# Attention scores and decay tiles contracted over all 128 rows, with one mask product for each tile

## The reference

```python
# mLSTM, 4 heads of 128 channels, chunks; here as one causal 256 x 256 weight
w = jnp.exp(d - m_t[..., None])              # d: sums of gate logs, -inf above the diagonal
qk = jnp.einsum('bhtd,bhsd->bhts', qj, kj) * w
# differential attention, 16 heads of 64 channels, in pairs
s = jnp.einsum('bhqd,bhkd->bhqk', qi, k_sh)
s = jnp.where(key_pos[None, :] <= qpos[:, None], s, -jnp.inf)
a = jax.nn.softmax(s, axis=-1)
diff = a[:, :, 0] - lam * a[:, :, 1]
```

## Time and profile before

| | |
|---|---|
| median of 3 runs | 2908.33 us (2906.72 to 2909.06) |
| span of the profiled execution, first to last instruction | 2907.0 us |
| the profiled execution's own time | not given apart from the span |
| TensorE busy | 2854.6 us (98%), 17894 products |
| VectorE, ScalarE, GpSimd busy | 67%, 56%, 12% |
| chain that ended last | TensorE 90%, VectorE 6%, ScalarE 2%, DMA 1% |
| granted TensorE clock, mean | 0.994 |

### The profile page before, as it was taken

How to read it: one execution, slowest core, us unless ns; L and a number is a source line. 1 busy time by engine, 2 the same in 40 slices (tenths; PEclk the granted TensorE clock), 3 DMA queues, 4 the chain that set the end, 5 groups by cost and what they waited for, 6 DMA issues and landing times.

```text
span 2907.0 us, 44463 instructions
## 1 busy us (share of the span) xinstructions
PE 2854.6 (98%) x17894; PEld 2553.7 (88%) x17894; DVE 1950.4 (67%) x3362; ACT 1633.4 (56%) x2794; POOL 342.4 (12%) x310
## 2 busy tenths in 40 slices
PE   8999999999989999999999999999999999999999
PEld 7888888788868877799999999999888889989997
DVE  6656765765566656759864898777555566756775
ACT  6544654754546555456655445776445555655663
POOL 0000000000000002000001444896000000000000
PEclk9999999999989999999999999999999999999999
DMA  6554556466334555445355554334555574526454
GB/s 211 195 175 152 177 196 210 135 206 217 126 116 151 202 187 163 130 141 176 102 164 183 178 185 162 131 131 159 189 193 198 188 238 133 163 85 209 147 188 153
DMA packets 304540, 490.33 MB, mean 169 GB/s; under 512 B 10880, under 2 KB 236544, under 8 KB 295632
## 3 DMA queue, kind: packets, MB, share of 16 engines
q1 hardware_dynamic: 303200, 480.09, 50.2%
q0 software_dynamic: 1136, 7.41, 0.7%
HBM read 485.36 MB, written 2.10 MB: 168 GB/s over the span
## 4 chain that ended last, share of the span: by engine, by line
PE 90%; DVE 6%; ACT 2%; DMA 1%; issue 1%; POOL 0%; SPq 0%; DVEq 0%; POOLq 0%; ACTq 0%
PE ps L608 30%; PE ps L538 11%; PE ps L542 11%; PE ps L539 11%; PE ps L687 10%; PE ps L686 5%; PE ps L559 2%; PE ps L1123 2%; DVE halves L1369 2%; PE ps L1158 1%; PE ps L1178 1%; PE ps L491 1%; DVE AR L2223 1%; PE ps L842 0%; DVE R L1369 0%
## 5 line engine op out<-in xcount | busy, mean ns | idle before, releaser
L2579 ACT ACTIVATE halves<-raw 128x1024 fp32r<-128x1024 f32 (+1 forms) x842 | 878.6, 1052 | 692.0 <-PE ps L608 335.8
L1369 DVE TENSOR_TENSOR halves<-raw,halves 128x1024 fp32r<-128x1024 f32 (+1 forms) x806 | 964.6, 1218 | 221.6 <-ACT halves L2579 218.8
L538 PE MATMUL ps<-XX,halves 128*128 128x256 f32 (+1 forms) x2360 | 586.5, 286 | 0.0
L539 PE MATMUL ps<-XX,halves 128*128 128x256 f32 (+1 forms) x2360 | 578.2, 283 | 0.0
L608 PE MATMUL ps<-halves,XX 128*128 128x512 f32 x2256 | 524.1, 392 | 5.5 <-DVE XX L1407 2.9
L608 PEld LDWEIGHTS ps<-halves,XX 128*128 128x128 f32 x2256 | 423.4, 189 | 100.3 <-issue 7.9
L538 PEld LDWEIGHTS ps<-XX,halves 128*128 128x128 f32 (+1 forms) x2360 | 451.4, 191 | 2.6 <-issue 2.0
L539 PEld LDWEIGHTS ps<-XX,halves 128*128 128x128 f32 (+1 forms) x2360 | 451.9, 191 | 0.2
L542 PE MATMUL ps<-XX,halves 128*128 128x256 f32 (+1 forms) x2360 | 331.5, 283 | 0.7 <-DVE halves L1369 0.7
L608 PE MATMUL ps<-halves,R 128*128 128x512 f32 x1404 | 323.0, 391 | 0.0
L687 PE MATMUL ps<-XX,halves 128*128 128x512 f32 x1264 | 317.8, 393 | 2.2 <-DVE XX L1407 2.2
(11 more groups left out here) (369 smaller groups left out, 3530.3 us busy)
## 6 DMA issues: line engine op xcount, KB each, us to landing
raw<-in_w_ffn_in SPq DMA_DIRECT2D x88, 1024.0 KB, 5.1
raw<-in_w_in SPq DMA_DIRECT2D x74, 1024.0 KB, 5.3
raw<-in_uT SPq DMA_DIRECT2D x64, 1024.0 KB, 4.8
raw<-in_peer_v SPq DMA_DIRECT2D x64, 1024.0 KB, 4.9
raw<-in_w_ffn_out SPq DMA_DIRECT2D x44, 1024.0 KB, 4.9
raw<-in_w_up SPq DMA_DIRECT2D x24, 1024.0 KB, 5.9
raw<-in_mlstm_w_in SPq DMA_DIRECT2D x12, 1024.0 KB, 5.4
raw<-in_w_down SPq DMA_DIRECT2D x12, 1024.0 KB, 4.9
```

The source lines that it names most:

```text
L538: mm(o[:, ts], hi[:, q, 0:M], xh[:, k0 + q, ts], start=first and q == 0, stop=False)
L539: mm(o[:, ts], hi[:, q, 0:M], xl[:, k0 + q, ts], start=False, stop=False)
L1369: te.tensor_tensor(lo, src, hi.bitcast(F32), ALU.subtract).then_inc(k.lo_made, 1)
L2579: act(hi, src, ACT.Copy).then_inc(k.hi_made, 1)
```

## The change

q is kept in two copies of 128 rows. In the one for the even head (or first half) rows 64 to 127 are zero, in the one for the odd head rows 0 to 63. The zeros come from the evacuation itself, which multiplies by a column that is zero in half of its rows. Each q evacuation of the differential attention and the third mixer (4 and 4, ScalarE) and of the second mixer (4, VectorE) so becomes two. Score products take both operands over 128 rows. The mLSTM's decay rows are kept in tiles of 128 rows, whose three used ones are filled with zeros by three VectorE memsets, and are transposed and spread over 128 rows. Wherever two bf16 mask products stood, one stands now: `diagonal` writes both diagonal blocks of the tile by one product of 256 columns.

```diff
+    def diagonal(self, b):
+        return self.ps[:, b, :].rearrange("p (a c) -> p a c", c=256)[:, :, 0:128]
...
+    def half_q(self, key, at, c, odd):
+        return self.odd_heads(key, c - c % 2)[:, c % 2, :] if odd else self.ar(at + c * 256, 256)
...
+    mkq, mqk = (bc(k.mask[:, o:o + 128].unsqueeze(1), [128, 2, 128]) for o in (0, 128))
...
-                    ins = transpose(ps[:, b, i * 8 + j * 4:i * 8 + j * 4 + 4],
-                                    r[:, j * 128:(j + 1) * 128], ident[0:4, 0:4])
+                    ins = transpose(ps[:, b, i * 256 + j * 128:i * 256 + j * 128 + 128],
+                                    r[:, j * 128:(j + 1) * 128], ident[:])
...
-                    sel = bc(ident[0:4, h:h + 1], [4, 128])
+                    sel = bc(ident[:, h:h + 1], [128, 128])
                     mm(ps[:, b, 0:256], sel, nA, start=True, stop=False)
-                    mm(ps[:, b, 0:256], identb[:], mkq2, start=False, stop=True)
-                    mm(ps[:, b, 256:384], sel, nA[:, 128:256], start=True, stop=False)
-                    ins = mm(ps[:, b, 256:384], identb[:], mkq, start=False, stop=True)
+                    mm(ps[:, b, 256:384], sel, nA[:, 128:256], start=False, stop=False)
+                    ins = mm(k.diagonal(b), identb[:], mkq, start=False, stop=True)
...
-                mm(ps[:, b, 0:128], qT[p0:p0 + 64, h, 0:128], kS[p0:p0 + 64, h, 0:128],
-                   start=True, stop=False)
-                mm(ps[:, b, 0:128], identb[:], mqk, start=False, stop=True)
-                mm(ps[:, b, 128:384], qT[p0:p0 + 64, h, 128:256], kS[p0:p0 + 64, h, :],
-                   start=True, stop=False)
-                ins = mm(ps[:, b, 128:384], identb[:], mqk2, start=False, stop=True)
+                mm(ps[:, b, 0:128], q[:, 0:128], kS[:, h, 0:128], start=True, stop=False)
+                mm(ps[:, b, 128:384], q[:, 128:256], kS[:, h, :], start=False, stop=False)
+                ins = mm(k.diagonal(b), identb[:], mqk, start=False, stop=True)
...
-            mm(ps[:, b, 0:128], qT[p0:p0 + 64, h // 2, 0:128], kT[p0:p0 + 64, h // 2, 0:128],
-               start=True, stop=True)
-            ins = mm(ps[:, b, 128:384], qT[p0:p0 + 64, h // 2, 128:256], kT[p0:p0 + 64, h // 2, :],
-                     start=True, stop=True)
+            mm(ps[:, b, 0:128], q[:, 0:128], kT[:, h // 2, 0:128], start=True, stop=True)
+            ins = mm(ps[:, b, 128:384], q[:, 128:256], kT[:, h // 2, :], start=True, stop=True)
...
-            mm(ps[:, b, 0:256], identb[:], mkq2, start=False, stop=False)
-            ins = mm(ps[:, b, 256:384], identb[:], mkq, start=False, stop=True)
+            ins = mm(k.diagonal(b), identb[:], mkq, start=False, stop=True)
...
-                mm(ps[:, b, o:o + n], identb[:], mqk2 if n == 256 else mqk, start=False, stop=False)
-                ins = mm(ps[:, b, o:o + n], qT[p0:p0 + 64, h // 2, q0:q0 + 128], kT[p0:p0 + 64, h // 2, 0:n],
-                         start=False, stop=n == 256)
+                mm(ps[:, b, o:o + n], q[:, q0:q0 + 128], kT[:, h // 2, 0:n], start=False, stop=False)
+            ins = mm(k.diagonal(b), identb[:], mqk, start=False, stop=True)
...
+        for i in (2, 3, 7):
+            te.memset(k.ar(6400 + 256 * i, 256), 0.0)
...
+                    if i == 0:
+                        te.tensor_scalar(k.odd_heads("m2", c), two(b), col("qn", 1), None, ALU.mult)
                     te.tensor_scalar((qT, kT)[i][:, c:c + 2, :], two(b), col(("qn", "kn")[i]), None, ALU.mult) \
...
+            act(k.odd_heads(odd, f), two(b), ACT.Copy, scale=col("hf", 1))
+            act(dst[:, f:f + 2, :], two(b), ACT.Copy, scale=col("hf")).then_inc(*main.done((key, f)))
```

More of the change, by code:

```diff
@@ L434, in hot, with odd_heads @@
         return (self.raw[:, 2, o:o + 1024].rearrange("p (o q i) -> p o q i", q=4, i=128) for o in (0, 1024))
+    def diagonal(self, b):
+        return self.ps[:, b, :].rearrange("p (a c) -> p a c", c=256)[:, :, 0:128]
+    def odd_heads(self, key, c):
+        off = {"df": 24576, "m2": 17408, "m3": 10496}[key] + c * 256
+        return self.ar(16448 if key == "m3" and c == 6 else off, 2, 256)
+    def half_q(self, key, at, c, odd):
+        return self.odd_heads(key, c - c % 2)[:, c % 2, :] if odd else self.ar(at + c * 256, 256)
     def gb(self, slot):
@@ L467, in tensor_engine @@
     ident, identb, wide_banks = k.ident, k.identb, k.wide_banks
-    mkq, mkq2, mqk2, mqk = k.mask[:, 0:128], k.mask[:, 0:256], k.mask[:, 128:384], k.mask[:, 256:384]
+    mkq, mqk = (bc(k.mask[:, o:o + 128].unsqueeze(1), [128, 2, 128]) for o in (0, 128))
     def weights():
@@ L740, in mlstm @@
         qT, kT, vx = k.ar(0, 4, 256), k.ar(1024, 4, 256), k.ar(4096, 2, 4, 257)
-        row = [k.AR[0:4, 6400 + 256 * i:6656 + 256 * i] for i in range(9)]
+        row = [k.ar(6400 + 256 * i, 256) for i in range(9)]
         a_, m_, nA = row[7], row[2], row[3]
@@ L845, in diff @@
     def diff(prev, kx, kv_ready):
-        qT, o_ = k.ar(0, 8, 256), k.ar(2048, 2, 1024)
+        o_ = k.ar(2048, 2, 1024)
         E, dT = k.AR[:, 8192:11264].rearrange("p (a b c) -> p a b c", b=4, c=384), k.ar(11264, 2, 384)
@@ L851, in scores @@
                 b = k.df_banks("s", h).take(pe, ("df", "s", h, c))
-                p0 = 64 * c
+                q = k.half_q("df", 0, h, c)
                 pe.wait_ge(*main.gone(("kv.k", h - h % 2)))
                 pe.wait_ge(*main.gone(("df.q", h - h % 2)))
-                mm(ps[:, b, 0:128], qT[p0:p0 + 64, h, 0:128], kS[p0:p0 + 64, h, 0:128],
-                   start=True, stop=False)
-                mm(ps[:, b, 0:128], identb[:], mqk, start=False, stop=True)
-                mm(ps[:, b, 128:384], qT[p0:p0 + 64, h, 128:256], kS[p0:p0 + 64, h, :],
-                   start=True, stop=False)
-                ins = mm(ps[:, b, 128:384], identb[:], mqk2, start=False, stop=True)
+                mm(ps[:, b, 0:128], q[:, 0:128], kS[:, h, 0:128], start=True, stop=False)
+                mm(ps[:, b, 128:384], q[:, 128:256], kS[:, h, :], start=False, stop=False)
+                ins = mm(k.diagonal(b), identb[:], mqk, start=False, stop=True)
                 filled(("df", "s", h, c), ins)
@@ L955, in mix2 @@
         qt, kt, vv = k.ar(0, 2, 1024), k.ar(2048, 2, 1024), k.ar(4096, 2, 1024)
-        qT, kT = k.ar(6144, 8, 256), k.ar(8192, 8, 256)
+        kT = k.ar(8192, 8, 256)
         E_, dT = k.ar(11520, 2, 384), k.ar(12288, 2, 384)
@@ L975, in score @@
         def score(h):
-            p0 = 64 * (h % 2)
+            q = k.half_q("m2", 6144, h // 2, h % 2)
             b = aux.take(pe, ("m2", "s", h))
             pe.wait_ge(*aux.gone(("m2.qk", 1, 6)))
-            mm(ps[:, b, 0:128], qT[p0:p0 + 64, h // 2, 0:128], kT[p0:p0 + 64, h // 2, 0:128],
-               start=True, stop=True)
-            ins = mm(ps[:, b, 128:384], qT[p0:p0 + 64, h // 2, 128:256], kT[p0:p0 + 64, h // 2, :],
-                     start=True, stop=True)
+            mm(ps[:, b, 0:128], q[:, 0:128], kT[:, h // 2, 0:128], start=True, stop=True)
+            ins = mm(ps[:, b, 128:384], q[:, 128:256], kT[:, h // 2, :], start=True, stop=True)
             filled(("m2", "s", h), ins)
@@ L1160, in mix3 @@
                 filled(("m3.rg", f, i), ins)
-        qT, kT, vv = k.ar(17536, 8, 256), k.ar(19584, 8, 256), k.ar(21632, 2, 1024)
+        kT, vv = k.ar(19584, 8, 256), k.ar(21632, 2, 1024)
         cx = k.part_at(26240, 384)[0:96, :]
@@ L1168, in score @@
         def score(h):
-            p0 = 64 * (h % 2)
+            q = k.half_q("m3", 17536, h // 2, h % 2)
             b = aux.take(pe, ("m3", "s", h))
@@ L1664, in decays @@
             v.wait_ge(*full["ml", "cols"])
-            te.tensor_copy(cc[:, 0:8], ps[:, b, 0:8])
-            te.tensor_copy(cc[:, 8:16], ps[:, b, 8:16]).then_inc(*aux.done(("ml", "cols")))
+            te.tensor_copy(cc[:, 0:16].rearrange("p (r h) -> p r h", h=4),
+                           ps[:, b, :].rearrange("p (r c) -> p r c", c=128)[:, :, 0:4]) \
+                .then_inc(*aux.done(("ml", "cols")))
             yield
@@ L2511, in vector_engine @@
         te.tensor_scalar(k.sel[g:g + 32, 32:48], k.ident[g:g + 32, g:g + 16], -1.0, None, ALU.mult)
-    te.memset(k.mask[:, 128:256], 0.0)
-    te.tensor_copy(k.mask[:, 256:384], mst[:, 0:128])
+    te.tensor_copy(k.mask[:, 128:256], mst[:, 0:128])
     te.tensor_copy(k.mask[:, 0:128], mst[:, 128:256]).then_inc(*step.mark("constants"))
@@ L2706, in evac, with halves_of @@
                 .then_inc(*main.done((key, f)))
+        return evac
+    def halves_of(key, dst, odd):
+        def evac(f):
+            a.wait_ge(*full[key, f])
+            b = main.of((key, f))
+            act(k.odd_heads(odd, f), two(b), ACT.Copy, scale=col("hf", 1))
+            act(dst[:, f:f + 2, :], two(b), ACT.Copy, scale=col("hf")).then_inc(*main.done((key, f)))
         return evac
@@ L2934, in diff @@
         kS = k.ar(20480, 8, 256)
-        keys, queries = out_of("kv.k", kS), out_of("df.q", qT, scale=0.125)
```

(12 more changed lines are left out.)

## The result

The changed kernel takes 2869.75 us (median of 4 runs, 2869.04 to 2875.41); the kernel before, on the same chip, 2907.52 us (4 runs). The ratio is 0.9882, 95% interval 0.987 to 0.9894, so 31 to 38 us less (the two medians differ by 37.8 us, the ratio says 34.3). Two later comparisons on other chips gave 0.9886 (0.9869 to 0.9902) and 0.9892 (0.9876 to 0.9909). Forecast were 2873.4 us and 34.9 us less.

The account below looks back on a forecast made before the run. TensorE's stream bounds the kernel (98% busy); gains of 14.4 + 10.7 + 5.5 + 1.8 + 2.5 = 34.9 us off the 2907.0 us span give 2872.1, plus 1.3 for the median: 2873.4 us. Range 2865.6 to 2888 us.

Parts of the forecast that it names:

- A score at 0.80 us: Differential attention: each of 16 scores falls from 1.42 to 0.80 us (bounds 0.75 and 0.85), gain 0.62 us each.
- The two rules that spoke against it: Trainium skill: different row groups run concurrently; weight loads overlap only across row groups or by second buffer, else 1.30 us a score.
- The clock in the scores: Differential attention: with fuller products the granted clock no longer falls, 1.00 expected from 765 to 776 us.
- Differential attention, 14.4 us: 16 scores there: 7.4 from scores, 2.9 from clock, 5.4 from the second stretch, less 1.3 us of waiting.
- The 2.9 and 3.3 us for the regained clock: Differential attention: time won if the two clock falls vanish, 6.2 us together.
- The wait ahead of the first output transposes: Differential attention: TensorE, 2.5 us early, waits for nearly full VectorE, charged 1.3 us (bounds 0 and 2.5).
- The last stretch: Differential attention's last pair: TensorE 6.4 us less, minus 0.5 for q's evacuation and 0.5 for VectorE, leaving 5.4 us.
- Third mixer, 10.7 us: Third mixer's 16 scores fall from 1.87 to 1.20 us, gain 0.67 us each.
- Second mixer, 5.5 us net: Second mixer's 16 scores gain 0.40 us each, 6.4 us, less 0.9 us for four more VectorE evacuations.
- mLSTM, 1.8 us: Four decay tiles fall from 1.32 to 0.82 us, 2.0 us, less 0.2 for full transposes; memsets hidden.
- State space, 2.5 us: Decay tiles fall from 0.42 to 0.30 us; 24 of 32 count, 2.9 us, taken as 2.5 (bounds 0 and 3.8).
- Rivals: Clock still falls 2879.6 us, 18%; VectorE's chain holds 2882.7, 17%; full-row loads in sight 2908, 4%; evacuating engines pace 2916.9, 3%.

Follow-up runs that it names:

- the fourth corner: The changed kernel with score products on half rows (64 and 4) and two 128-column masks, both copies of q kept: 2911.62 us, ratio 1.0019.
- its stretched version: The changed kernel with half rows and one mask, each differential score's three products made six times over: span 2985.9 us, one run.
- the second profile of the kernel before: The kernel before run once more, unedited: 2904.43 us (one run), span of the profiled execution 2902.6 us.
- the one-copy kernel: The changed kernel without the 12 added q evacuations, odd heads' scores taken with the even heads' copy: 2869.22 us, ratio 0.9878.
- Neither variant that was meant to cure it: Changed kernel with two masks in the first eight state-space tiles: 2871.6 us; the same with ScalarE making the second mixer's even q copy: 2870.2 us.

## Why the prediction was right, point by point

- **The bound.** TensorE's stream set the time: TensorE's busy time fell by 36 us and the span by 33.4. The sum was right for partly compensating reasons, by the points below: the gains by rows and masks were put too low in three of the five places, the clock lost in new places was put at nothing, and the clock regained was read from one execution with long falls.
- **A score at 0.80 us.** Measured 0.76, within the bounds of 0.75 and 0.85. The full-row products of the mLSTM were the right rows to read it from the earlier trace rows. The discount for a load behind the mask was not needed. With half rows and one mask the same score costs 1.07 us, with two masks and full rows 0.82 to 0.88, with both 1.36.
- **The two rules that spoke against it.** Full-row loads hide as rows 5 and 6 showed; what is in sight with half rows is the load of the second pass, 0.33 against 0.22 us, and as much again at changes of row count. The Trainium skill says that changing the tiling mode drains TensorE (TensorEngine Tiling (Array Packing), Key Properties). The extra time at the changes agrees with this, three times 0.10 us for each half-row product that stands alone, but a drain and a load left in sight look the same in these start times. The first of the two rules, that products on different row groups run concurrently, was not tested by any run: in every kernel full-row work stands between products of the two halves. The 1.42 us of the prediction therefore do not speak against it, and a kernel that issues both halves' products side by side remains an untested rival to the zeros.
- **The clock in the scores.** Forecast to hold, and it held in every profile of the changed kernel. But the reason given, fuller products, is only half of it: in the one profile with half rows and one mask it held too, over the ordinary scores. It fell in the scores where half rows and a mask between every two products came together, in both profiles of the kernel before and in the fourth corner, and in neither of the two profiles with only one of these (half rows with one mask, full rows with two). Whether one mask is enough in every execution is not shown: half of that kernel's runs had a lower mean clock than the profiled one, and its stretched version fell once.
- **Differential attention, 14.4 us.** Measured 15.8 between the first profiles, but 11.2 against the second profile of the kernel before. The 2.9 and 3.3 us for the regained clock were read from an execution with long falls; that it was the one compared is luck. The wait ahead of the first output transposes was mis-sized, 0.51 us instead of 0.16 where 1.3 us more were charged. The last stretch came out as worked, 5.4 us (2.2 us against the second profile), but not by the rows: half rows with one mask give 5.2.
- **Third mixer, 10.7 us.** Measured 12.4. The score took 1.16 to 1.19 us, near the forecast 1.20. Mis-sized was the cost before: rows 8 have 1.87 us, but every other score of the kernel before took 1.95 to 1.97, and the work behind a score started 0.02 to 0.06 us later than now.
- **Second mixer, 5.5 us net.** Measured 4.6. The round is 0.34 us shorter, not 0.40; the evacuations cost 0.68 us, not 0.9.
- **mLSTM, 1.8 us.** Measured 2.5; a tile takes 0.76 us instead of the forecast 0.82, and the product behind it 0.44 instead of 0.49. The memsets were hidden: TensorE began the transposes at 241.3 us, against 241.5 before.
- **State space, 2.5 us.** The step that failed in the profiled executions: -0.5 us. The 0.12 us a tile are there (neighbouring tiles start 0.30 us apart, 1381.85 after 1381.55 us, against 0.42 in rows 9), and 2.8 us in an execution that kept its clock, that of the one-copy kernel. The price came with the 3.3 us of the fall, which the prediction named only as what would make it wrong, "a clock fall at a new place". It stood in three profiles of three of the changed kernel. With the 1.4 us of the fall at 543 us, which two of these three have, it makes 4.7 us, about the distance between the profile's 33.4 us and the median's 37.8, if the shorter runs are those without it. Their mean clock was higher, as said above; where they gained it is not shown, since they left no trace.
- **Rivals.** None came about. The evacuations cost 0.7 us out of 7.8.

What stays open is why the clock falls at 1386 us. It fell in six of seven profiles with one mask in all state-space tiles, in one of two with two masks in the first eight, and in none of four with two masks everywhere. That speaks for the thinner work in front of ScalarE's exponentials, but does not show it. Neither variant that was meant to cure it beat the changed kernel.

## What to carry to other kernels

Read the price of a TensorE product from start to start in its own surroundings: a half-row fp32 product between others of other row counts cost 0.30 us more than the same columns over full rows, two of them in a row 0.31 to 0.34 together, and zeros in the other half were nearly free, 0.7 us for all the second copies. Short products between two others cost more than their columns, and the price of two such habits does not add: here the second mask cost 14 us on half rows and 4 on full ones, 12 and 6 at equal clock. Take the second profile of the kernel before too: the falls of one execution were more than twice as long as those of the other and cost 4.6 us more in the differential attention alone. When TensorE's work gets thinner, look for a new fall of the granted clock before counting the gain: 3.3 us of it went that way in one stage.

## What the runs showed that was not expected

- Half-row scores kept the 2.4 GHz level for 25 us on end, but once at 1.2 GHz they stayed there for 17 us, until full-row work came (one stretch of one execution).
- The falls are tied to places in the program and differ in length between executions: 769 to 776 and 823.5 to 834 us in one profile of the kernel before, 772 to 775 and 823 to 826.5 in the other. Not all come every time: the one at 543 us stood in two of three profiles of the changed kernel.
- The runs of the changed kernel form two groups, about 2869.7 and 2874 us. With 0.15% between them, medians of four runs of the same program came out at 2869.75, 2871.7 and 2874.5.
